# Head norms in three batches inside the attention loop, residual panels begun in pairs, weight splits spread out, and a second panel loaded and summed ahead of the first statistic

## What is computed

```
mx  = silu(c) @ ada_w[i] + ada_b[i]              # and mc from c_ctx: shift, scale, gate, twice each
ax  = rms_norm(hx, g) * (1 + scale) + shift      # ac alike, for the context

# layer 1 of the first block, 8 heads, values 128 wide, keys are 256 tokens + 256 context
p = softmax(q k^T / 8)                           # two maps a head
o = (p[0] - lam * p[1]) @ v
o = rms_norm(o, sub_g) * (1 - lam_init)          # the head norm
hx = hx + gate * (concat(o) @ odd_w_out)

# feed-forward of the second block, 2816 = 22 * 128 hidden channels
u = conv3(h @ w_up) + conv_b ; g, up = split(u)
x = x + (silu(g) * up) @ w_down
```

## Time and profile before

| | us |
|---|---|
| runs without a profile (3): median, lowest, highest | 1799.64, 1798.38, 1804.41 |
| the profiled execution, its own time | 1807.0 |
| its span, first to last instruction | 1805.2 |
| PE busy in the span | 1692.3 (94%) |
| DVE busy | 1042.1 (58%) |
| ACT busy | 833.3 (46%) |
| POOL busy | 81.6 (5%) |

### The profile page before, as it was taken

How to read it: one execution, slowest core, us unless ns; L and a number is a source line. 1 busy time by engine, 2 the same in 40 slices (tenths; PEclk the granted TensorE clock), 3 DMA queues, 4 the chain that set the end, 5 groups by cost and what they waited for, 6 DMA issues and landing times.

```text
span 1805.2 us, 30854 instructions
## 1 busy us (share of the span) xinstructions
PE 1692.3 (94%) x12092; PEld 1494.7 (83%) x12092; DVE 1042.1 (58%) x1972; ACT 833.3 (46%) x1546; POOL 81.6 (5%) x90
## 2 busy tenths in 40 slices
PE   3999989999999989997799999988999998989998
PEld 1985566888888879974799999868999998689998
DVE  4436644634343454358565566665877647668675
ACT  3327744523232342236344455574545546745443
POOL 2100001000000012110000001000000000000000
PEclk8999999999999999999999999999999999999999
DMA  8717763333333333347256663613666536046662
GB/s 250 212 47 254 238 175 104 108 104 94 94 101 98 94 117 94 113 135 220 82 152 180 178 181 106 182 35 106 182 182 190 149 110 179 21 139 176 180 191 86
DMA packets 406255, 254.48 MB, mean 141 GB/s; under 512 B 8448, under 2 KB 405024, under 8 KB 406112
## 3 DMA queue, kind: packets, MB, share of 16 engines
q1 hardware_dynamic: 404576, 248.80, 46.9%
q0 software_dynamic: 1536, 3.71, 0.8%
HBM read 251.36 MB, written 1.11 MB: 140 GB/s over the span
## 4 chain that ended last, share of the span: by engine, by line
PE 88%; DVE 6%; ACT 3%; issue 2%; DMA 1%; SPq 0%; DVEq 0%; ACTq 0%
PE bank L2151 72%; PE bank L2361 3%; PE bank L2372 2%; PE bank L2274 2%; PE bank L2382 2%; PE bank L2130 2%; PE bank L2162 1%; DVE parts L1118 1%; PE bank L2356 1%; DMA H<-ctx_t 1%; PE bank L2388 1%; ACT parts L1301 1%; PE bank L2397 1%; PE bank L2307 1%; ACT PR L1493 0%
## 5 line engine op out<-in xcount | busy, mean ns | idle before, releaser
L2151 PE MATMUL bank<-AT,parts 128*128 128x256 f32 (+1 forms) x4704 | 683.1, 308 | 14.7 <-DVE AT L1104 7.5
L2151 PEld LDWEIGHTS bank<-AT,parts 128*128 128x128 f32 x4704 | 639.2, 193 | 56.9 <-issue 18.2
L1301 ACT ACTIVATE parts<-raw 128x1024 fp32r<-128x1024 f32 (+1 forms) x368 | 368.7, 1041 | 333.4 <-PE bank L2151 323.2
L1118 DVE TENSOR_TENSOR parts<-raw,parts 128x1024 fp32r<-128x1024 f32 (+1 forms) x368 | 435.0, 1214 | 149.5 <-ACT parts L1301 149.1
L2151 PE MATMUL bank<-HID,parts 128*128 128x256 f32 (+1 forms) x2592 | 401.4, 317 | 9.1 <-DVE HID L1800 9.1
L2151 PEld LDWEIGHTS bank<-HID,parts 128*128 128x128 f32 x2592 | 368.2, 193 | 40.4 <-DVE HID L1800 9.7
L2151 PE MATMUL bank<-parts,AT 128*128 128x256 f32 x2112 | 269.3, 291 | 12.7 <-DVE WORK L1943 7.1
L2151 PEld LDWEIGHTS bank<-parts,AT 128*128 128x128 f32 x2112 | 265.6, 199 | 15.2 <-DVE WORK L1943 7.6
L2031 DVE SCALAR_TENSOR_TENSOR H<-bank,MOD,H 128x256 f32<-128x256 f32 x120 | 52.6, 480 | 158.7 <-PE bank L2151 158.7
L1301 ACT ACTIVATE TOK<-bank 128x512 f32<-128x512 f32 (+2 forms) x160 | 71.2, 487 | 148.7 <-PE bank L2151 119.9
L2016 DVE TENSOR_TENSOR PR<-PR 128x512 f32<-128x512 f32 x48 | 33.2, 691 | 113.8 <-ACT PR L1545 113.8
(11 more groups left out here) (200 smaller groups left out, 1258.9 us busy)
## 6 DMA issues: line engine op xcount, KB each, us to landing
raw<-mlp_w SPq DMA_DIRECT2D x128, 512.0 KB, 4.2
raw<-ada_w SPq DMA_DIRECT2D x96, 512.0 KB, 4.8
raw<-w_up SPq DMA_DIRECT2D x88, 512.0 KB, 4.7
raw<-w_in SPq DMA_DIRECT2D x32, 512.0 KB, 4.7
raw<-w_down SPq DMA_DIRECT2D x32, 512.0 KB, 4.3
raw<-odd_w_in SPq DMA_DIRECT2D x24, 512.0 KB, 4.1
raw<-w_out SPq DMA_DIRECT2D x16, 512.0 KB, 5.0
raw<-even_w_in SPq DMA_DIRECT2D x12, 512.0 KB, 10.1
```

The source lines that it names most:

```text
L1118: ng.tensor_tensor(chunk_part(c, 1), chunk_raw(c), chunk_part(c, 0).bitcast(F32), ALU.subtract)\
L1301: return nc.scalar.activation(o, i, ACT.Copy)
L2151: ins = MM(out, stay, move, start=opens and kt == 0 and i == 0, stop=kt == kts - 1 and i == 2 and stops)
```

## The change

Five edits to the list, and code that follows from them:

1. **Start.** The row of panel 4 and the sums of panels 0 and 4 stand ahead of the statistic, no longer behind it. SP issues the two loads of `H` behind four half panels of `ada_w` (n == 4), no longer behind two. The two chunks of the first `even_w_in` panel are split behind `apply` 0, no longer behind `apply` 1.
2. **Fill.** The adaptive rows of both attention loops are given out over three steps less (`n - 3`).
3. **Splits.** The first four chunks of `even_w_out` and of `odd_w_out` are split at four units, eight apart, no longer all at one.
4. **Head norms.** Root and scale of the head outputs come in three batches (jobs 0 to 7, 8 to 11, 12 to 15): in steps 11 and 12, in steps 15 and 16, and after the last value. The units `turn_o` stand in steps 13, 14, 17 and behind the last batch; the low parts are units of their own (`out_low`). High and low parts go to `HID`, whose memory holds the used query and key columns of that layer, and no longer to `AT`, which still holds the turned queries and keys.
5. **Pairs.** The first two panels of `odd_w_out` and of `w_down` in the last group are computed together: all tiles but the last two of panel 0, the same of panel 1, then the last two of panel 0 and of panel 1. Each bank is opened with a product with zeros (`open_bank`). For `odd_w_out` the last `turn_o` stands between the first two pieces. In the last `conv` unit the chunks are split ahead of the hidden tiles' high and low parts.

```diff
@@ attention(jobs, fill, between)
-            while put_in < len(fill) and put_in * n < (i + 1) * len(fill):
+            while put_in < len(fill) and put_in * (n - 3) < (i + 1) * len(fill):
                 put(fill[put_in])
                 put_in += 1
+            for stand in between.get(i, ()):
+                stand()
@@ plan()
     row(0)
+    row(4)
+    sums(0, 4)
     norm("n1", 0, 2 * N, "norm1_g", shift=0, scale=1)
     st = units[-1]
-    row(4)
-    sums(0, 4)
@@
-              list(ada(1, (3, 4, 5))))
-    for i in range(4):
-        add("turn_o", ("turn_o", 1, i), layer=1, ft=i)
+              list(ada(1, (3, 4, 5))),
+              {11: [lambda: heads_root(0, 8)], 12: [lambda: heads_scale(0, 8)], 13: [lambda: turn_out(0)],
+               14: [lambda: out_low(0), lambda: turn_out(1)], 15: [lambda: out_low(1), lambda: heads_root(8, 12)],
+               16: [lambda: heads_scale(8, 12)], 17: [lambda: turn_out(2)], 18: [lambda: out_low(2)]})
+    heads_root(12, 16)
+    heads_scale(12, 16)
+    turn_out(3)
+    out_low(3)
@@
+        elif c.name in ("even_w_out", "odd_w_out") and before[-1].name == "ada_w" and split[i - SPLIT].users[-1] < loaded:
+            at = min(at + 8, c.users[0] - 2)
         if c.name == "even_w_in" and c.c0 < 2 * PW:
-            at = max(at, units.index(index[("apply", 0, 1 if c.c0 == 0 else 3)]))
+            at = max(at, units.index(index[("apply", 0, 0 if c.c0 == 0 else 3)]))
@@ sync
-                if n == 2:
+                if n == 4:
                     sp.dma_start(H[:, :, 0:N], ...)
...
@@ vector, last conv of the last group
+                    elif last_group(pos):
+                        low_part(dve, V, x.splits[0])
...
+                        for c in x.splits[1:] if last_group(pos) else ():
+                            low_part(dve, V, c)
@@ tensor
+            def in_two_parts(x, y, at, turned=None):
+                for of in (x, y):
+                    bank_free(of)
+                    for c in of.chunks:
+                        chunk_ready(c)
+                    open_bank(of)
+                    resid_columns(of, range(at))
+                    if of is x and turned is not None:
+                        turn_outputs(turned)
+                for of in (x, y):
+                    resid_columns(of, range(at, of.kts)).then_inc(bank_filled, 1)
```

More of the change, by code:

```diff
@@ L221, in statistic, with attention @@
         index[st.key] = st
-    def attention(jobs, fill=()):
+    def attention(jobs, fill=(), between={}):
         fill = list(fill)
@@ L490, in plan @@
     for pos, x in enumerate(units):
-        if x.kind not in ("ada_row", "ahead", "post", "tail", "apply", "mix", "soft", "flush", "prep", "rstd", "final"):
+        if x.kind not in ("ada_row", "ahead", "post", "tail", "apply", "mix", "soft", "flush", "heads_root", "heads_scale", "out_low", "prep", "rstd", "final"):
             x.u = u
@@ L998, in turned_o_from @@
             return b if x.layer == 0 else b.rearrange("p (a t) -> p a t", a=2)
-        def turn_o_waits(x):
-            return [last_value[x.layer].u]
         def turn_o_pairs(x, b):
@@ L1130, in last_hidden, with last_group @@
             return units[pos].up == 1 and units[pos + 1].kind == "resid" and units[pos + 1].g == units[pos].g
+        def last_group(pos):
+            return last_hidden(pos) and units[pos].g == 2
         def hidden_exact(x):
@@ L1637, in _ @@
                         square(pos, st, kt)
-                if k != "conv" or last_hidden(pos):
+                if k != "conv" or last_hidden(pos) and not last_group(pos):
                     high_parts(x)
@@ L2116, in _ @@
                     late = None
-                if (k != "conv" or last_hidden(pos)) and not (k == "stat" and x.dst == "AT"):
+                if (k != "conv" or last_hidden(pos) and not last_group(pos)) and not (k == "stat" and x.dst == "AT"):
                     low_parts(dve, V, x, 0)
@@ L2242, in one_and_half, with turn_outputs, resid_columns, moved @@
                 last.then_inc(bank_filled, 1)
+            def turn_outputs(x):
+                bank_free(x)
+                pe.wait_ge(head_done, 2 * TB * (x.ft + 1))
+                for o, i in turn_o_pairs(x, bank[:, x.u % BANKS, :]):
+                    last = nc.tensor.transpose(o, i, ident)
+                last.then_inc(bank_filled, 1)
+            def resid_columns(x, tiles):
+                for c in range(2):
+                    last = split_product(bank[:, x.u % BANKS, c * N:c * N + N], x, x.kts, c * P, P,
+                                         lambda kt, part: moved(x, kt, part), True, lambda kt: resid_wait(pe, x, kt),
+                                         tiles, False, c == 1)
+                return last
+            def in_two_parts(x, y, at, turned=None):
[9 more added lines that the diff above has]
+                    resid_columns(of, range(at, of.kts)).then_inc(bank_filled, 1)
+            def moved(x, kt, part):
+                w = 2 * N if x.wide else N
+                if x.src == "HID":
+                    lo = x.g % 2 * N if not x.wide else 0
+                    return HID[:, part, kt, lo:lo + w]
+                if x.kind == "resid" and x.key[1] == "odd_w_out":
+                    return outs(part)[:, kt, :]
+                return AT[:, part, kt, 0:w]
+            two_parts = {("resid", "odd_w_out", 0, n, None) for n in range(2)} | {("resid", "ffn", l, n, None)
+                                                                                for l in range(2) for n in range(2)}
             first_of = {}
```

82 lines of the change are left out of this document (49 added, 33 removed).

## The result

The changed kernel takes 1815.94 us (median of 4 runs, 1815.13 to 1819.11), the kernel before 1799.99 (1798.38 to 1804.41): a ratio of 1.0087, interval 1.0071 to 1.0102. It is 16 us slower. The sign was forecast, the size was not: +5.0 was said, and 1815.94 lies above the range.

A forecast was written before the change was run, and what follows sets the result against it. PE, busy 94%, was taken as the bound, with time won only where it idles or clocks low. Terms 1.6 - 1.0 + 4.0 + 0.4 = +5.0 took 1799.6 to 1804.6 us, range 1801 to 1809 (1792 to 1810 overall).

The forecast's parts named there:

- DVE's waits stay the same in sum: End of layer 1's attention: DVE's waits, 6.8 us before, would be 6.9 after, while its work grows by 5.9.
- Start, +1.6: Start: H 3.0 us later delays the dense stretch, earlier splits release part; +1.6 us, bounds -1.3 and +3.0.
- Layer 0, -1.0: End of layer 0's attention: -5.4 from spread splits, +2.1 for moved row products, +2.3 for remaining waits; -1.0 us.
- Layer 1, +4.0: End of layer 1's attention and first panels: third panel +3.3 later, 0.7 for lower clock; +4.0 us, bounds -5 and +8.
- The pair: First panels of odd_w_out: third panel waits for its chunks until 886.7, after a first panel at 871.5; 2.3 us new waiting.
- Feed-forward, +0.2 apiece: Last group, both feed-forwards: 3.0 us idle before the second panel's chunks, third panel 0 to +1.0 later; +0.2 us each.
- The clock is lost in the new short waits: Rival: new waits bring 1.2 GHz, first panels lose 3 us more; about +9, 1808.6 us; chance 0.11.
- Head norms for free: Rival, end of layer 1: splits and batches fill DVE's idle time, term about -3, sum -6.3, 1793.3 us; chance 0.25.
- the point that I gave: Layer 1, steps 11 to 17: the faster rival decides once DVE's idle time falls under 2 us.

The follow-up runs named there:

- spread_fill: Kernel before with the splits of even_w_out and odd_w_out spread and the attention loops' fill given out over n - 3 steps: 1.0080.
- after_lag: Changed kernel with DVE's low part of odd_w_out's four splits one step after ACT's high part: 1.0055 of the kernel before.
- best2: Kernel before with even_w_out's splits spread, zero products in feed-forward and first-normed-tile waits, identity turns ahead of head outputs: 1790.39 us, 0.9936.

## Why the prediction was wrong

One step failed above all: that in layer 1 DVE's waits stay the same in sum. They grew from 7.1 to 11.5 us, and the term came out at +8.4 instead of +4.0. Layer 0 and the feed-forwards came out 1.6 and 1.5 above what was said, and the two medians lie another 4 us further apart than the two profiled executions.

**Start, +1.6.** Right as a mechanism and in the profiles: H is issued 3.6 late and the squares begin 3.8 late (3.0 was said), the x360 run starts 1.7 late in the mean of 6 against 13 executions and ends 1.3 late. The time of the part alone doesn't show it (-0.07%, interval -0.22 to +0.08).

**Layer 0, -1.0.** Measured +0.6. Each half by itself was nearly right: the spread wins 3.6 where 3.1 was said (-5.4 + 2.3; no row stood behind the 2.3), and the earlier fill costs 1.5 where 2.1 was said. But the two together leave +0.5 instead of the sum of -2.1, and up to +4.5 in other executions. Their meeting was missed.

**Layer 1, +4.0.** This term failed, at +8.4 (6.2 to the first panel, 2.2 from there to the sums). By its steps: mix 9 starts 1.4 later against before where 2.1 was said; DVE's work is 27.9 instead of 28.9; its idle time is 11.5 instead of 6.9. That is the step that was wrong: "the waits stay about the same in sum". It has two parts.

The smaller: the four single waits ahead of low parts are 6.2 where 5.2 was said.

The larger: beside them the forecast kept 1.7 of waits, "in the last two steps". The kernel before had 5.2 beside its 1.9: 1.40 and 1.71 for values, 0.53 and 0.45 for scores, and some 1.1 in gaps too short for the view. The changed kernel has 5.4: 1.56 and 2.29 for values, 0.45 for a score, and the rest short. So 3.5 us of waits that stood in the trace were put at nothing, as if the batches' work would fill them, and no reason was given. The sum looked unchanged, 6.9 against 6.8, only because the new waits had taken their place. Of the 3.9 for values, 1.2 is PE at 1.2 GHz (eight products in 1.71 and 1.64 instead of 1.06).

From the last mix to the first panel it took 5.1 instead of 3.3, all at a granted 0.50. The pair came as worked out: 15.3 against 15.2.

The view that the batches' work is the bulk of this term holds for the batches alone (4.8 more from mix 9 to the last mix), but not in the changed kernel, where that stretch is 9.6 longer. Taking the batches out shortens it by 2.2, undoing the early fill by 3.6 and making the low parts lag by 5.7. There the spread splits, with the fill, make the loop long, and the batches stand in part in waits that these make.

**Feed-forward, +0.2 apiece.** The places were right (idle 3.09; second panel's split; third panel 1.70 behind). The clock was not: the 48 products took 8.37 and 7.39, so 2.6 and 1.6 of lower clock. That is about the "1.2 to 2.4" for which the forecast gave 0 to +1.0; the time of the part alone is +0.14%, 2.5 us for both. Zero products in the wait bring it to +0.02%, with intervals that overlap.

**The rivals.** "The clock is lost in the new short waits" had 0.11 and was nearest: 0.50 granted behind waits of 2.87, 5.26 and 3.41 in the loop. What spoke against it, "it was 0.55 only after the long wait", left out a part of the same view. The clock had been 0.50 in the loop too, from 847 to 853, behind the wait of 6.34; only behind that did it stay high, with PE less busy still. Two stretches of the kernel before:

```profile
850.00:853.00 3.00, 3.00 (x14) 2.04 (x12) 1.42 (x8) 2.18 (x7) 0.00 (x0) 0.50 1.20 291
...
862.00:865.00 3.00, 0.74 (x7) 0.55 (x5) 1.22 (x6) 1.33 (x6) 0.00 (x0) 1.00 0.00 0
```

So a high clock behind short waits said little about what new waits of 3 to 5 us would do. The Trainium skill, page "TensorE: Matmul & The Clock Gate", section "A second HAM failure mode: psum-queue depth-cycling", has that frequent short idles make the clock swing; the stretches of 3 us from 850 to 871, at 0.50, 0.78, 1.00, 0.86, 0.57, 1.00 and 0.50, agree with it. The rival's size, +9, was too small too. "Head norms for free" decided itself by the point that I gave: DVE's idle time was never under 2 us, and yet the loop was longer. Idle time of DVE was no sign of slack, as much of it lay ahead of instructions behind which the next mix stands. That criterion was wrong.

**The sum.** Stages of the profiled executions: +12.1. Median of the runs: +16. The profiled execution before was itself 7.0 us above its median (1807.0), the one after 3.2 (1819.1); that accounts for the difference.

**Open.** That fill and spread meet so hard (0.80% against 0.34% as a sum) is shown, and that waits before low parts and a clock of 0.50 come with it. Why is not: only for the last two steps of spread_fill is the clock's share known, 1.3 us each, and after_lag changed waits and clock at once. Nor is it known why layer 0 ranges between +0.5 and +4.5 with the same order.

## What to carry to other kernels

- Work spread over the steps of a pipelined loop isn't free where it joins two engines in a ring within a step. Ask of each piece: does its producer stand behind what this step makes, and its consumer ahead of what the next step needs? If so, let the consumer lag by a step, or leave the pieces together where one wait serves all.
- Test edits in pairs: here two parts of +0.1% and +0.2% made +0.8%, and one of +0.35% was worth some -0.28% beside them.
- A long wait of PE (3 to 5 us here) has a second price behind it. Products of zero in two kinds of such waits and turns of the identity in a third were worth 0.64% together with one moved split (best2).

## What the runs showed of the hardware

- Behind waits of PE of 2.87, 3.41 and 5.26 us the granted clock was 0.50 (1.2 GHz). The same 48 products behind the same wait of 3.09 took between 6.92 and 8.37 in ten places of five executions, and 5.91 with PE kept busy in the wait. I had not expected that spread.
- The clock stayed at 0.50 over 18 us (848 to 866 in spread_fill) while PE was busy 3.6 to 4.3 of every 6 us.
- The same wait of 1.7 us ahead of a turn stands at a clock of 1.00 in the kernel before (857.03 and 860.25) and at 0.50 in spread_fill (864.06 and 868.56). There the low clock held on through waits behind which the high one didn't fall.
